# Where the key and query norms of a cross-attention stand: beside the mixer's output projection and the second query block

## The chip, the cores and the metric

The kernel runs on one core of a Trainium2 chip. The metric is the device time of one execution in microseconds, the median of several runs. Below, PE is TensorE, DVE is VectorE, ACT is ScalarE, POOL is GpSimd and SP is SyncE, which only issues loads here.

## What is computed

Two transformer blocks on 256 tokens of width 1024, in float32. Each has two layers. The change touches the second block alone, and there one step of each layer: the cross-attention to a memory of 256 rows, with the projection that ends the mixer ahead of it.

```python
def mem_cross_attention(h, mem_n, w_q, w_kv, q_gain, k_gain, w_out):
    q = rmsnorm_2((h @ w_q).reshape(Bn, S, X_HEADS, X_HEAD_DIM), q_gain)
    k, v = jnp.split(mem_n @ w_kv, 2, axis=-1)
    k = rmsnorm_2(k.reshape(Bn, M, X_HEADS, X_HEAD_DIM), k_gain)
    s = jnp.einsum('bqhd,bkhd->bhqk', q, k) * (X_HEAD_DIM ** -0.5)
    ...
for l in range(DEPTH):
    x = x + mixer(h)                      # ends with  @ w_out, "mix_out"
    x = x + mem_cross_attention(rmsnorm_2(x, norm_mem_q[l]), rmsnorm_2(mem, norm_mem_kv[l]), ...)
    x = x + swiglu(rmsnorm_2(x, norm_ffn[l]), ffn_w_gu[l], ffn_w_down[l])
```

There are 4 heads of width 256, so each head's keys (and queries) fill two tiles of 128 rows by 256 tokens, and a head's norm sums the squares of both.

## The kernel before, in words

**Weights and tiles.** Every weight matrix is streamed in blocks of 1024 x 512 (2 MB) into `raw`, which has two slots. A block is cut in four quarters. ACT copies a quarter to `w_hi` (`split_high`, L1406), rounded to a shorter format; DVE subtracts to get the remainder `w_lo` (`split_low`, L1927). One output tile (128 columns by 256 tokens) is 24 matmuls: 8 parts of the inner dimension times three products of high and low parts (`tile_t`, L602). A quarter of the next block may overwrite `w_hi` only when the tile that used the quarter is summed, so `split_high(b + 1, t)` waits for tile t of block b. SP loads block b when `split_low` of block b-2 is complete, since they share a slot.

**Order.** There is no scheduler. Each engine runs its own list, written out by hand, strictly in order, and the engines meet at semaphores. An instruction that waits holds up all that stands behind it on its engine.

**The steps in question**, for each layer of the second block:

1. `mix_out`, two blocks, 8 tiles. For each tile DVE adds the tile to `hidden` (`add_tile`, L1978), ACT writes the high part of the normed operand and the squares (`finish_chunk`, L1424 and L1428) and then splits a quarter (L1406); DVE writes the low part (`finish_low`, L1947) and splits.
2. `xq`, first block, 4 tiles. The token norm is summed on PE after two of them (L674), ACT turns it into `rs`, and DVE scales the tiles into `xq`.
3. `xq`, second block, 4 tiles, with the four key norms between them.
4. the four query norms, with nothing between.
5. attention: 8 units of scores, softmax, transposes and values; then `x_out`.

**One head norm** (`head_norms`) is a chain over four engines: ACT squares a head's two tiles (`square`, L1453, 128x512), PE sums them (`hn_sum`, L698), ACT takes Ln and Exp (`scale`, L1463 and L1466), DVE scales the two tiles (L1999). On ACT the list is square(0), and then for each i: square(i+1), scale(i), `between(i)`. On PE it is hn_sum(i), `between(i)`; on DVE scale(i), `between(i)`. What `between` issues is how other work is put beside the norms.

The scores of the attention wait until all norms of queries and keys are scaled (`hn_scaled`).

## Time and profile before

| | us |
|---|---|
| median of 3 runs | 1709.52 (1707.77 to 1711.32) |
| the profiled execution | 1702.04 |
| its span | 1700.3 |
| PE busy | 1604.6 (94%) |
| DVE busy | 1128.2 (66%) |
| ACT busy | 807.7 (48%) |
| layer 0: first tile of `mix_out` read, to the first tile of `x_out` read | 965.45 to 1044.25 |
| layer 1: the last tile of the first `xq` block read, to the first tile of `x_out` read | 1436.14 to 1481.37 |

All positions are microseconds from the start of the span. The profiled execution is 7.5 us quicker than the median of the runs, so a sum made in the trace is carried to the median as a difference. PE is the busy engine and DVE and ACT have room, which makes the places where PE stands still the ones to look at.

### The profile page before, as it was taken

Reading aid. Unit: us, or ns where it says so; the run is one execution under the profiler, and the core shown is the slowest. Engines: PE = TensorE matmul, PEld = TensorE weight load, DVE = VectorE, ACT = ScalarE, POOL = GpSimd, SP = SyncE. Lnnn points to the kernel's source line nnn. Section 1 sums busy time; section 2 is a strip of 40 time slices with the busy share of each in tenths; the row PEclk is TensorE's granted clock in tenths of the full one; section 3 lists DMA queues with packets and bytes.
Section 4 is the critical chain, followed back from the end, with each engine's and each line's share of the span. In section 5 each row is a group of like instructions: output and inputs, shape, how many; then the busy total and the mean of one; then the engine's idle time right before and its main releaser. Section 6 shows DMA issues by size and latency. Waiting matters only on the chain.

```text
span 1700.3 us, 31460 instructions
## 1 busy us (share of the span) xinstructions
PE 1604.6 (94%) x12572; PEld 1523.9 (90%) x12572; DVE 1128.2 (66%) x2032; ACT 807.7 (48%) x1402; POOL 188.7 (11%) x200
## 2 busy tenths in 40 slices
PE   6988999999998899999998989999989999899998
PEld 5876898999997699999996688999989999899997
DVE  5884644777675667777677755666677566566666
ACT  4446225444354554445554455544455555554443
POOL 2670501000031020002000011000020002010000
PEclk9998898999999999999998799999999999999999
DMA  6420002454553045544542142555535444256552
GB/s 212 148 81 20 1 2 96 152 180 166 183 189 132 1 149 199 197 171 176 194 153 99 50 150 80 169 199 198 171 114 188 141 158 152 75 171 199 186 174 88
DMA packets 125813, 236.56 MB, mean 139 GB/s; under 512 B 2614, under 2 KB 50025, under 8 KB 125689
## 3 DMA queue, kind: packets, MB, share of 16 engines
q1 hardware_dynamic: 124393, 230.29, 39.2%
q0 software_dynamic: 1296, 4.53, 0.8%
q8 instruction: 89, 1.46, 0.4%
q14 instruction: 35, 0.29, 0.1%
HBM read 233.76 MB, written 1.05 MB: 138 GB/s over the span
## 4 chain that ended last, share of the span: by engine, by line
PE 83%; DVE 10%; ACT 3%; issue 2%; SPq 0%; DMA 0%; POOL 0%; DVEq 0%; ACTq 0%; POOLq 0%
PE ps L602 46%; PE ps L649 6%; PE ps L648 6%; PE ps L647 6%; PE ps L610 5%; DVE w_lo L1927 3%; PE ps L780 3%; PE ps L741 2%; PE ps L698 2%; PE ps L929 1%; PE ps L754 1%; PE ps L911 1%; DVE u_lo L1947 1%; DVE hidden L1978 1%; ACT w_hi L1406 1%
## 5 line engine op out<-in xcount | busy, mean ns | idle before, releaser
L1406 ACT ACTIVATE w_hi<-raw 128x1024 fp32r<-128x1024 f32 x440 | 460.2, 1051 | 291.8 <-PE ps L649 137.3
L1927 DVE TENSOR_TENSOR w_lo<-raw,w_hi 128x1024 fp32r<-128x1024 f32 x440 | 540.7, 1229 | 10.4 <-ACT w_hi L1406 10.2
L602 PE MATMUL ps<-u_hi,w_hi 128*128 128x256 f32 (+1 forms) x1544 | 446.9, 289 | 14.9 <-DVE u_lo L1947 8.6
L602 PE MATMUL ps<-u_hi,w_lo 128*128 128x256 f32 (+1 forms) x1544 | 440.8, 285 | 0.0
L602 PE MATMUL ps<-u_lo,w_hi 128*128 128x256 f32 (+1 forms) x1544 | 440.4, 285 | 0.0
L602 PEld LDWEIGHTS ps<-u_hi,w_hi 128*128 128x128 f32 x1544 | 294.4, 191 | 21.6 <-DVE u_lo L1947 10.6
L602 PEld LDWEIGHTS ps<-u_hi,w_lo 128*128 128x128 f32 x1544 | 294.8, 191 | 0.0
L602 PEld LDWEIGHTS ps<-u_lo,w_hi 128*128 128x128 f32 x1544 | 293.8, 190 | 0.5
L602 PE MATMUL ps<-a_hi,w_hi 128*128 128x256 f32 (+1 forms) x800 | 230.0, 288 | 5.3 <-DVE a_lo L1942 2.3
L602 PE MATMUL ps<-a_lo,w_hi 128*128 128x256 f32 (+1 forms) x800 | 227.2, 284 | 0.0
L602 PE MATMUL ps<-a_hi,w_lo 128*128 128x256 f32 (+1 forms) x800 | 227.1, 284 | 0.0
L647 PE MATMUL ps<-a_hi,w_hi 128*128 128x256 f32 (+1 forms) x688 | 195.1, 284 | 0.8 <-DVE hidden L1978 0.8
L649 PE MATMUL ps<-a_hi,w_lo 128*128 128x256 f32 (+1 forms) x688 | 195.6, 284 | 0.0
L648 PE MATMUL ps<-a_lo,w_hi 128*128 128x256 f32 (+1 forms) x688 | 195.3, 284 | 0.0
L1978 DVE TENSOR_TENSOR hidden<-ps,hidden 128x256 f32<-128x256 f32 (+1 forms) x272 | 115.9, 426 | 116.5 <-PE ps L649 60.5
L602 PEld LDWEIGHTS ps<-a_hi,w_hi 128*128 128x128 f32 x800 | 152.9, 191 | 7.3 <-DVE a_lo L1942 2.8
L1966 DVE TENSOR_TENSOR work<-ps,rs 128x256 f32<-128x256 f32 (+1 forms) x153 | 65.4, 428 | 140.6 <-PE ps L602 119.7
L602 PEld LDWEIGHTS ps<-a_hi,w_lo 128*128 128x128 f32 x800 | 153.2, 191 | 0.0
L602 PEld LDWEIGHTS ps<-a_lo,w_hi 128*128 128x128 f32 x800 | 152.2, 190 | 0.4
L647 PEld LDWEIGHTS ps<-a_hi,w_hi 128*128 128x128 f32 x688 | 129.9, 189 | 1.0 <-DVE w_lo L1927 1.0
L649 PEld LDWEIGHTS ps<-a_hi,w_lo 128*128 128x128 f32 x688 | 130.0, 189 | 0.0
L648 PEld LDWEIGHTS ps<-a_lo,w_hi 128*128 128x128 f32 x688 | 129.3, 188 | 0.0
(377 smaller groups left out, 2359.6 us busy)
## 6 DMA issues: line engine op xcount, KB each, us to landing
raw<-in_w_ff_dram SPq DMA_DIRECT2D x32, 2048.0 KB, 8.5
raw<-in_ffn_w_gu_dram SPq DMA_DIRECT2D x44, 1024.0 KB, 7.5
raw<-in_ffn_w_down_dram SPq DMA_DIRECT2D x10, 2048.0 KB, 7.8
raw<-in_xa_w_kv_dram SPq DMA_DIRECT2D x8, 2048.0 KB, 8.0
raw<-in_od_w_in_dram SPq DMA_DIRECT2D x6, 2048.0 KB, 8.0
raw<-in_w_in_ab_dram SPq DMA_DIRECT2D x5, 2048.0 KB, 7.8
raw<-in_ev_w_in_dram SPq DMA_DIRECT2D x5, 2048.0 KB, 8.1
raw<-in_xa_w_q_dram SPq DMA_DIRECT2D x4, 2048.0 KB, 7.8
```

What stands on the lines that cost most here:

```text
L602: mm = pe.matmul(bank[:, 0:n], wx[:, q, k * P:(k + 1) * P], x[ux][:, k, ts], start=k == 0 and i == 0, stop=k == KD - 1 and i == 2)
L610: mm = pe.matmul(bank[:, at:at + n_quarters * n].rearrange("p (q n) -> p q n", n=n), x[ux][:, k, ts], wx[:, q:q + n_quarters, k * P:k * P ...
L647: pe.matmul(tile_bank[t % 4][:, 0:n], hi[:, k, cols], a[0][:, at_k, ts], start=k == 0, stop=False)
L648: pe.matmul(tile_bank[t % 4][:, 0:n], hi[:, k, cols], a[1][:, at_k, ts], start=False, stop=False)
L649: mm = pe.matmul(tile_bank[t % 4][:, 0:n], lo[:, k, cols], a[0][:, at_k, ts], start=False, stop=k == chunks - 1)
L698: mm = pe.matmul(banks[u_ % 2][:, 0:n], matrix, hn_sq[:, u_ % 2, i * n:(i + 1) * n], start=i == 0, stop=i == tiles - 1)
L741: mm = pe.matmul((b4, b5)[v % 2][0:x["nq"], 0:x["nk"]], q, k, start=c == 0, stop=c == len(x["q"]) - 1)
L780: mm = pe.matmul(bank[x["parts"], r * P:r * P + x["nq"]], vs[r], at_pt[0:rows, v % 2, c, 0:x["nq"]], start=c == 0, stop=c == len(x["keys"] ...
L1406: act.activation(quarter(w_hi, b, q), raw_quarter(b, q), ACT.Copy).then_inc(high_split, 1)
L1927: dve.tensor_tensor(quarter(w_lo, b, q), raw_quarter(b, q), quarter(w_hi, b, q).bitcast(F32), ALU.subtract)\
L1966: dve.tensor_tensor(target, tile_bank[t][:, 0:n], rs[:, ts] if scale is None else scale, ALU.mult)\
L1978: dve.tensor_tensor(hidden[:, k, ts], tile_bank[t][:, 0:ts.stop - ts.start], hidden[:, k, ts], ALU.add)\
```

## The change

Three lists are edited alike, those of PE, ACT and DVE. The key norms move from the second `xq` block to `mix_out`: after the first tile of `mix_out`, the key norms are issued with the other seven tiles between them, two, two, two and one. The second `xq` block now has the query norms beside it: its first tile is issued, then the query norms with one tile behind the first of them and two behind the second; nothing stands behind the third and fourth. The arithmetic is the same, and no instruction is added or removed.

```diff
+        def mix_fill(i):
+
+            return 2 * i + 1, min(2 * i + 3, 8)
+
+        def xq_fill(i):
+
+            return ((1, 2), (2, 4), (4, 4), (4, 4))[i]
...
 (PE)
-                out_product(f"mix_out{layer}", REAL, ready)
-                b = first_of(f"xq{layer}")
-                block_t(b, u, REAL, ready=chunks_ready(), norm=REAL)
-
-                head_norms([(2, SEQ, ones)] * 4, between=lambda t: tile_t(b + 1, t, u, REAL))
-                head_norms([(2, SEQ, ones)] * 4)
+                mix_tiles(0, 1)
+                head_norms([(2, SEQ, ones)] * 4, between=lambda i: mix_tiles(*mix_fill(i)))
+                block_t(first_of(f"xq{layer}"), u, REAL, ready=chunks_ready(), norm=REAL)
+                second_tiles(0, 1)
+                head_norms([(2, SEQ, ones)] * 4, between=lambda i: second_tiles(*xq_fill(i)))
                 pe.wait_ge(hn_scaled, hn[0])
...
 (ACT)
-                residual(f"mix_out{layer}", f"memq{layer}", REAL)
+                def mix_tiles(lo, hi):
+                    for n in range(lo, hi):
+                        b, t = phases[f"mix_out{layer}"].first + n // 4, n % 4
+                        finish_chunk(n, f"memq{layer}", (tile_read, tile_at[b] + t + 1), REAL)
+                        split_high(b + 1, t)
+
+                def second_tiles(lo, hi):
+                    for t in range(lo, hi):
+                        split_high(phases[f"xq{layer}"].first + 2, t)
+
+                mix_tiles(0, 1)
+                pair_norms(xk, f"xkv{layer}", lambda i: mix_tiles(*mix_fill(i)))
                 norm_rs(rs[:, REAL], SEQ)
                 stream(f"xq{layer}", nothing, 0, 1)
-                for x, name, fill in ((xk, "xkv", True), (xq, "xq", False)):
-                    first, after = tile_at[phases[f"{name}{layer}"].first], phases[f"xq{layer}"].first + 2
...
-                               between=(lambda t: split_high(after, t)) if fill else None)
+                second_tiles(0, 1)
+                pair_norms(xq, f"xq{layer}", lambda i: second_tiles(*xq_fill(i)))
...
 (DVE)
-                residual(f"mix_out{layer}", f"memq{layer}", REAL)
-                rms_ready()
+                def mix_tiles(lo, hi):
+                    for n in range(lo, hi):
+                        b, t = phases[f"mix_out{layer}"].first + n // 4, n % 4
+                        add_tile(n, t, tile_at[b] + t, REAL)
+                        if n >= 1:
+                            finish_low(n - 1, f"memq{layer}", REAL)
+                        split_low(b + 1, t - 1)
...
+                mix_tiles(0, 1)
+                pair_norms(xk, "xa_k", lambda i: mix_tiles(*mix_fill(i)))
+                finish_low(KD - 1, f"memq{layer}", REAL)
+                rms_ready()
+                stream(f"xq{layer}", project_xq, 0, 1)
+                second_tiles(0, 1)
+                pair_norms(xq, "xa_q", lambda i: second_tiles(*xq_fill(i)))
```

How the lists come out is shown at two places. First ACT at the start of `mix_out` in layer 0. `u_hi<-hidden` and `squares<-hidden` are `finish_chunk`, `w_hi<-raw` is `split_high`, `work<-mx` is `square`, and the two `work` rows behind it are `scale`. Before:

```order
L1424 ACTIVATE u_hi<-hidden,gains 128x256 [waits tile_read]
L1428 ACTIVATE squares<-hidden 128x256 [waits sum_added]
L1406 ACTIVATE w_hi<-raw 128x1024 [waits tile_summed,raw_in1]
L1424 ACTIVATE u_hi<-hidden,gains 128x256 [waits tile_read]
L1428 ACTIVATE squares<-hidden 128x256 [waits sum_added]
```

and in the changed kernel, whose lines stand 15 further down:

```order
L1439 ACTIVATE u_hi<-hidden,gains 128x256 [waits tile_read]
L1443 ACTIVATE squares<-hidden 128x256 [waits sum_added]
L1421 ACTIVATE w_hi<-raw 128x1024 [waits tile_summed,raw_in1]
L1468 ACTIVATE work<-mx 128x512 [waits hn_summed,tile_read] x2
L1478 ACTIVATE work<-ps,cst 128x256 [waits hn_scaled,hn_summed]
L1481 ACTIVATE work<-work 128x256 [waits hn_ln]
L1439 ACTIVATE u_hi<-hidden,gains 128x256 [waits tile_read]
```

The squares of the first two heads' keys now stand behind the chunk and the quarter of the first tile. On PE the sum that needs them stands between the first tile and the second (`work,cst` is `hn_sum`):

```order
L610 MATMUL ps<-a_hi,w_hi 128x256 [waits operand_split]
L610 MATMUL ps<-a_lo,w_hi 128x256
L610 MATMUL ps<-a_hi,w_lo 128x256
L706 MATMUL ps<-work,cst 128x256 [waits hn_ln,hn_squared]
L706 MATMUL ps<-work,cst 128x256
L610 MATMUL ps<-a_hi,w_hi 128x256 [waits tile_read,low_split]
```

Before, the fourth row followed directly on the third of a tile, with the waits `tile_read,low_split`; now PE first waits for the squares.

The second place is ACT from the first `xq` block to the query norms, layer 0. Before:

```order
L1406 ACTIVATE w_hi<-raw 128x1024 [waits tile_summed,raw_in1]
L1406 ACTIVATE w_hi<-raw 128x1024 [waits tile_summed] x3
L1453 ACTIVATE work<-mx 128x512 [waits hn_summed,tile_read] x2
L1463 ACTIVATE work<-ps,cst 128x256 [waits hn_scaled,hn_summed]
L1466 ACTIVATE work<-work 128x256 [waits hn_ln]
L1406 ACTIVATE w_hi<-raw 128x1024 [waits tile_summed,raw_in0]
```

and now:

```order
L1421 ACTIVATE w_hi<-raw 128x1024 [waits tile_summed,raw_in1]
L1421 ACTIVATE w_hi<-raw 128x1024 [waits tile_summed] x3
L1421 ACTIVATE w_hi<-raw 128x1024 [waits tile_summed,raw_in0]
L1468 ACTIVATE work<-mx 128x512 [waits hn_summed,tile_read] x2
L1478 ACTIVATE work<-ps,cst 128x256 [waits hn_scaled,hn_summed]
L1481 ACTIVATE work<-work 128x256 [waits hn_ln]
```

The row with `raw_in0` is the first quarter of the next weight, `x_out`: it waits for the load of that block. It stood behind the first norm's squares, and stands ahead of them now.

## Rows read from the trace of the kernel before

**Rows 1.** The page, busy time by engine: us, share of the span, instructions.

```profile
PE 1604.6 (94%) x12572; PEld 1523.9 (90%) x12572; DVE 1128.2 (66%) x2032; ACT 807.7 (48%) x1402; POOL 188.7 (11%) x200
```

**Rows 2.** The page, the chain that ended last, shares by engine.

```profile
PE 83%; DVE 10%; ACT 3%; issue 2%; SPq 0%; DMA 0%; POOL 0%; DVEq 0%; ACTq 0%; POOLq 0%
```

**Rows 3.** Timeline of DVE, layer 0: start, us, line, tile [idle before <- releaser].

```profile
965.45 0.42 DVE L1978 TENSOR_TENSOR hidden<-ps,hidden 128x256 f32<-128x256 f32 x1 [1.76 <-PE ps L602]
...
985.33 0.42 DVE L1978 TENSOR_TENSOR hidden<-ps,hidden 128x256 f32<-128x256 f32 x1 [0.89 <-PE ps L602]
...
997.82 0.42 DVE L1966 TENSOR_TENSOR mx<-ps,rs 128x256 f32<-128x256 f32 x1 [0.23 <-PE ps L602]
...
1001.58 0.88 DVE L1999 SCALAR_TENSOR_TENSOR mx<-mx,late,work 128x256 f32<-128x256 f32 x2 [2.20 <-ACT work L1466]
1003.45 0.42 DVE L1966 TENSOR_TENSOR mx<-ps,rs 128x256 f32<-128x256 f32 x1 [0.99 <-PE ps L602]
...
1014.57 0.42 DVE L1966 TENSOR_TENSOR mx<-ps,rs 128x256 f32<-128x256 f32 x1 [0.92 <-PE ps L602]
...
1022.32 0.88 DVE L1999 SCALAR_TENSOR_TENSOR mx<-mx,late,work 128x256 f32<-128x256 f32 x2 [0.45 <-ACT work L1466]
...
1044.25 0.42 DVE L1978 TENSOR_TENSOR hidden<-ps,hidden 128x256 f32<-128x256 f32 x1 [1.99 <-PE ps L602]
```

**Rows 4.** Timeline of ACT, layer 0.

```profile
966.63 1.04 ACT L1406 ACTIVATE w_hi<-raw 128x1024 fp32r<-128x1024 f32 x1
...
997.82 1.06 ACT L1406 ACTIVATE w_hi<-raw 128x1024 fp32r<-128x1024 f32 x1 [1.78 <-PE ps L602]
998.78 1.13 ACT L1453 ACTIVATE work<-mx 128x512 f32<-128x512 f32 x2
```

**Rows 5.** Timeline of PE, layer 0.

```profile
988.21 0.39 PE L602 MATMUL ps<-u_hi,w_hi 128*128 128x256 f32 x1 [0.44 <-DVE u_lo L1947]
...
999.45 1.13 PE L698 MATMUL ps<-work,cst 128*128 128x256 f32 x4 [1.67 <-ACT work L1453]
...
1023.25 5.52 PE L741 MATMUL ps<-mx 128*128 128x256 f32 x16 [1.93 <-DVE mx L1999]
```

**Rows 6.** The load of `x_out`'s first block, layer 0: issue, time to landing, and DMA share (second to last column) around its end.

```profile
994.68 0.37 SPq L566 DMA_DIRECT2D raw<-in_xa_w_out_dram  x1
```

```profile
raw<-in_xa_w_out_dram SPq DMA_DIRECT2D x1, 2048.0 KB, 7.8
```

```profile
1000.00:1002.00 2.00, 2.00 (x17) 1.95 (x16) 0.42 (x2) 0.89 (x2) 0.00 (x0) 1.00 0.94 347
```

**Rows 7.** The same steps in layer 1: timeline of DVE, and the chain.

```profile
1436.14 0.42 DVE L1966 TENSOR_TENSOR mx<-ps,rs 128x256 f32<-128x256 f32 x1 [0.23 <-PE ps L602]
...
1481.37 0.43 DVE L1978 TENSOR_TENSOR hidden<-ps,hidden 128x256 f32<-128x256 f32 x1 [1.96 <-PE ps L602]
```

```profile
1461.57 1.14 PE ps L741 x4
```

**Rows 8.** PE after its longer waits (timeline), and granted clock (third to last column) of windows.

```profile
19.19 0.56 PE L602 MATMUL ps<-u_hi,w_hi 128*128 128x272 f32 x1 [4.20 <-DVE w_lo L1927]
...
542.35 0.56 PE L685 MATMUL ps<-cst,rs_mem 128*128 128x128 f32 x2 [2.47 <-ACT rs_mem L1438]
...
922.75 0.49 PE L741 MATMUL ps<-mx 64*128 64x128 f32 x4 [3.10 <-DVE mx L2010]
...
1347.82 0.39 PE L602 MATMUL ps<-a_hi,w_hi 128*128 128x256 f32 x1 [2.04 <-DVE a_lo L2533]
```

```profile
18.00:22.00 4.00, 2.81 (x12) 2.84 (x13) 3.20 (x3) 2.40 (x3) 3.02 (x5) 1.00 1.04 310
542.00:544.00 2.00, 1.28 (x4) 0.86 (x5) 0.16 (x1) 0.91 (x3) 0.00 (x0) 0.63 0.00 0
924.00:926.00 2.00, 1.50 (x5) 0.98 (x5) 1.89 (x5) 0.91 (x4) 0.00 (x0) 0.70 0.00 0
1348.00:1352.00 4.00, 4.00 (x22) 4.00 (x23) 0.00 (x0) 3.37 (x3) 0.00 (x0) 0.57 0.00 0
1024.00:1028.00 4.00, 4.00 (x12) 2.97 (x12) 1.43 (x5) 1.13 (x4) 0.00 (x0) 0.60 0.00 0
```

More of the change, by code:

```diff
@@ L1365, in _ @@
                     u, a = a, u
-                out_product(f"mix_out{layer}", REAL, ready)
-                b = first_of(f"xq{layer}")
-                block_t(b, u, REAL, ready=chunks_ready(), norm=REAL)
-                head_norms([(2, SEQ, ones)] * 4, between=lambda t: tile_t(b + 1, t, u, REAL))
-                head_norms([(2, SEQ, ones)] * 4)
+                def mix_tiles(lo, hi):
+                    for n in range(lo, hi):
+                        tile_t(first_of(f"mix_out{layer}") + n // 4, n % 4, a, REAL, ready if n == 0 else None)
+                def second_tiles(lo, hi):
+                    for t in range(lo, hi):
+                        tile_t(first_of(f"xq{layer}") + 1, t, u, REAL)
+                mix_tiles(0, 1)
[3 more added lines that the diff above has]
+                head_norms([(2, SEQ, ones)] * 4, between=lambda i: second_tiles(*xq_fill(i)))
                 pe.wait_ge(hn_scaled, hn[0])
@@ L2714, in _, with mix_tiles, second_tiles, pair_norms @@
                                gate=[lr[:, c] for c in range(8)], ts=REAL, between=lambda i: memory_tiles(*od_fill(i)))
-                residual(f"mix_out{layer}", f"memq{layer}", REAL)
-                rms_ready()
+                def mix_tiles(lo, hi):
+                    for n in range(lo, hi):
+                        b, t = phases[f"mix_out{layer}"].first + n // 4, n % 4
[3 more added lines that the diff above has]
+                        split_low(b + 1, t - 1)
                 def project_xq(i, t, gt):
                     scaled(xq[:, 4 * i + t], t, gt, REAL)
-                def second_xq(t):
-                    b = phases[f"xq{layer}"].first + 1
-                    project_xq(1, t, tile_at[b] + t)
-                    split_low(b + 1, t - 1)
-                stream(f"xq{layer}", project_xq, 0, 1)
-                for x, g, between in ((xk, "xa_k", second_xq), (xq, "xa_q", None)):
+                def second_tiles(lo, hi):
+                    for t in range(lo, hi):
+                        b = phases[f"xq{layer}"].first + 1
+                        project_xq(1, t, tile_at[b] + t)
+                        split_low(b + 1, t - 1)
+                def pair_norms(x, g, between):
                     head_norms([([x[:, 2 * h + r] for r in range(2)], [col(g, 2 * layer + r) for r in range(2)],
                                  [x[:, 2 * h + r] for r in range(2)]) for h in range(4)], between=between)
+                mix_tiles(0, 1)
[5 more added lines that the diff above has]
+                pair_norms(xq, "xa_q", lambda i: second_tiles(*xq_fill(i)))
                 attention([dict(nq=P, nk=SEQ, kind=None, parts=slice(0, P), chunks=slice(2 * h, 2 * h + 2),
```

8 lines of the change are left out of this document (6 added, 2 removed).

## The prediction

> **What bounds the kernel now.** I read the page first. PE is busy 94% of the span [rows 1], and the chain that ended last lies on PE for 83% of its length, with 10% on DVE and 3% on ACT [rows 2]. So what this change can win is PE time that stands idle or runs slowly between the mixer's projection and the attention, and what it can lose is the same. After that I read the timelines of DVE, ACT and PE of that stretch in layer 0, and compared the same stretch of layer 1.
>
> The clearest clock of PE's progress is when DVE reads a finished tile. I call that moment R. In `mix_out` the first tile is read at 965.45 and the eighth at 985.33 [rows 3]: 19.88 / 7 = 2.84 us a tile, without a pause. In the second `xq` block the first tile is read at 1003.45 and the fourth at 1014.57 [rows 3]: 11.12 / 3 = 3.71 us for a tile with a key norm's sum ahead of it. One sum between tiles thus costs 0.87 us when its squares are ready.
>
> When they are not ready PE waits. The last tile of the first `xq` block is read at 997.82; ACT splits a quarter at the same moment, starts the squares 0.96 us later at 998.78 [rows 4], and PE starts the sum at 999.45, 0.67 us after that and after an idle 1.67 us [rows 5]. The next tile is read 4.00 us after the sum's start, at 1003.45. The same wait comes once more before the query norms. After the last tile is read at 1014.57, the four query norms run alone. The last scaling starts at 1022.32 and the attention at 1023.25 [rows 3, 5], 0.93 us later. From 1014.57 that is 8.68 us in which PE does little. From the read at 997.82 to the attention it is 25.43 us, and in layer 1 from 1436.14 to 1461.57 also 25.43 us [rows 7]. The two layers are alike.
>
> **The change, part by part.** I count for one layer, in the trace's own time.
>
> *Tiles beside the key norms.* The first tile of `mix_out` is read at R. ACT's quarter for it starts at 966.63, which is R + 1.18 [rows 3, 4], and the order puts the key squares behind it: they start at R + 1.18 + 0.96 = R + 2.14, and PE can start the sum at R + 2.14 + 0.67 = R + 2.81. Until then PE has nothing else, since its list has the sum ahead of the second tile. The second tile is read 4.00 us after the sum starts, at R + 6.81 instead of R + 2.84: **+3.97**. The other three sums find their squares ready, because ACT makes them one head ahead, and cost 0.87 each: **+2.61**. Their own scale steps on ACT and DVE take about 1 us each and lie beside two tiles of 2.84. DVE gets to the tile behind a scaling up to 0.7 us late and has caught up by the next; four banks of PSUM cover that. So the last of the eight tiles is read 6.58 us later than now.
>
> Behind it PE waits for the last low part of the operand: 0.44 us today [rows 5]. The last scaling delays DVE by about 0.2 us more there: **+0.2**. If DVE and ACT were later than I follow them, this term would grow to about 1 us. The other bound is -0.4, if the wait were gone. The four key sums themselves are not new work: they leave the second `xq` block, which is counted next.
>
> *Query norms beside the second `xq` block.* Counted from the read at 997.82. The first tile of the second block needs no sum ahead of it any more and is read at 1000.66. Now the order matters again: ahead of the query squares ACT has the first quarter of `x_out`, which waits for that tile and for its load. The load is issued at 994.68 and lands 7.8 us later [rows 6], at 1002.48; the DMA engines are 94% busy until 1002. Today nobody sees this, since the quarter is wanted at 1003.5 only. The issue does not move relative to 997.82, because it hangs on the fourth quarter of the first `xq` block. So the quarter starts at 1002.48, the squares at +0.96, the sum at +0.67: 1004.11. PE has been idle since 1000.6, for 3.5 us. Then the reads: 1004.11 + 4.00 = 1008.11, + 3.71 = 1011.82 with the second sum, + 2.84 = 1014.66 for the fourth tile. The third sum follows at once. The last head's squares stand behind that tile's quarter on ACT: the last sum starts at 1014.66 + 0.96 + 0.67 = 1016.29. From a sum's start to the scaling on DVE it is 2.13 us (999.45 to 1001.58 [rows 3, 5]), and 0.93 more to the attention: 1016.29 + 2.13 + 0.93 = 1019.35. Against 1023.25: **-3.90**. Most of it is the tail behind the last tile, 4.69 us instead of 8.68, less the longer wait at the head.
>
> The Trainium skill bears on the landing: its page "DMA: Bandwidth & Descriptors", section "Anatomy of one DMA — SWDGE (gpsimd) path", fits 2.0 us fixed plus bytes over 436 GB/s for a load issued from GpSimd. For 2 MB that would be an estimated 6.8 us by that page, a landing 1.0 us sooner and a sum lower by 1.0 us a layer. These loads are issued by SP and take 7.8, and I go by the row.
>
> *Sum without the clock.* +3.97 + 2.61 + 0.2 - 3.90 = +2.9 a layer, **+5.8** for both.
>
> *The clock.* The change turns two waits of 1.67 us a layer into one of 2.8 and one of 3.5, both with dense tiles behind. What such a wait does to the granted clock can be read elsewhere in this trace. After a wait of 3.10 us the window from 924 has 0.70; after 2.47 us the one from 542 has 0.63; after 2.04 us four microseconds from 1348 have 0.57 in dense tiles; after 4.20 us at the start of the program the clock stays at 1.00 [rows 8]. So three of these four waits were followed by a stretch at the lower level, 1.2 instead of 2.4 GHz. The price in dense tiles is 4.0 x 0.43 = 1.7 us. Four new waits in the two layers, three of them punished: **+5.1**; the bounds are 0 and +6.9. One dip may go: in layer 0 the attention begins at 0.60 [rows 8] and takes 21.00 us from its start to the first `x_out` tile (1023.25 to 1044.25), in layer 1 without a dip 19.80 (1461.57 to 1481.37) [rows 3, 5, 7]. Less stands still ahead of it now, so I take it away: **-1.2**; the bounds are -1.2 and +1.2, the latter if layer 1 gets one.
>
> Total: +5.8 + 5.1 - 1.2 = **+9.7 us**. The profiled execution goes from 1702.04 to about 1711.7, and the median from 1709.52 to 1719.2; I say 1719.
>
> **The rivals.** All times are on the median's scale. About 0.2%, 3.4 us, is what a measurement of this kernel can tell from no change.
>
> *No dip comes.* The waits of 1.67 us in this stretch leave the clock alone today, and the longer ones may be spared as well, as the wait of 4.20 us was. Then only the order counts: +5.8 - 1.2 = +4.6, 1714. For it: a wait of 1.93 us led to a dip in layer 0 and not in layer 1. Against it: three of four.
>
> *Every wait is punished, and the attention's dip stays.* +5.8 + 6.9 = +12.7, 1722. In this kernel it means that the second `mix_out` tile and the second tile of the second `xq` block both run at 0.5 in both layers. [...]
>
> *The load is not late.* If the `x_out` block has landed by 1000.66, the wait at the head of the query norms is 1.8 us shorter, as long as today's, and brings no dip. For that the landing would have to take 6 us instead of 7.8. Then +5.8 - 3.6 = +2.2, with about one dip left at `mix_out` and the attention's gone: +2.7, 1712, no measurable change. The DMA row speaks against it.
>
> *Faster: the sums find their squares.* If PE does not stand at the two new places, because ACT gets to the squares before PE ends the tile ahead, each of the two places costs only 0.87 for a sum. That takes 3.97 - 0.87 = 3.1 away at `mix_out` and 3.65 at `xq` (the sum at 1000.46 instead of 1004.11): 2.9 - 6.75 = -3.9 a layer, and 1709.5 - 7.7 - 1.2 = 1701. It decides from the point where the two waits together are 2.9 us shorter a layer than I find. Against it stands the order: on ACT both squares come behind work that waits for that very tile.
>
> *The change does nothing*: excluded, the order has it on all three engines.
>
> **How the numbers follow.** Forecast, two or three dips, +8 to +10: 0.50. No dip, 1714: 0.20. All dips, 1722: 0.14. The load not late, 1712: 0.10. Faster, 1701: 0.06. The first three are slower by more than 3.4 us: 0.84; same 0.10; faster 0.06. The range reaches from 1711, which takes in the case without dips and half of the next, to 1726, which has all dips, the +1 of the operand's wait in both layers and a spread of the runs of about 2. What is left out is the faster case, half of the one with an early load, and 0.05 above.
>
> **What would show it.** In the changed profile, in both layers: (1) a wait of PE of about 2.8 us behind the first `mix_out` tile, ended by ACT's squares, and 26.5 us from the first to the eighth read instead of 19.9; (2) a wait of about 3.5 us behind the first tile of the second `xq` block, ended by the same line, with ACT itself waiting for the load of `x_out`; (3) 4.7 us from the last `xq` tile's read to the attention instead of 8.7, and 21.5 us instead of 25.4 from the read ahead of the block; (4) clock windows below 1.0 behind most of the waits. I am wrong if the wait at (1) is under 2 us, if ACT doesn't wait for the load at (2), or if later stages give the time back, for which I see no slack since PE is dense behind the attention.

## The result

| | before | changed |
|---|---|---|
| median | 1709.52 us (1705.08 to 1713.9, 7 runs) | 1724.79 us (1718.66 to 1726.82, 7 runs) |
| ratio | 1 | 1.0079, 95% interval 1.0059 to 1.0098 |
| profiled execution | 1702.04 | 1726.82 |

The change costs 0.8%: 15.3 us between the medians. The prediction was 1719 in a range of 1711 to 1726.

The page of the changed kernel begins with these lines: its span, the busy time by engine, and, further down, the chain that ended last.

```profile
span 1725.0 us, 31460 instructions
...
PE 1618.4 (94%) x12572; PEld 1536.4 (89%) x12572; DVE 1128.1 (65%) x2032; ACT 809.4 (47%) x1402; POOL 188.8 (11%) x200
...
PE 81%; DVE 11%; ACT 3%; issue 2%; DMA 1%; SPq 0%; POOL 0%; DVEq 0%; ACTq 0%; POOLq 0%
```

The instructions are as many as in [rows 1]. DVE and ACT are as busy as they were. PE is busy 13.8 us longer with the same work, at a lower clock (the windows below show where), and the chain now has 1% on a DMA where [rows 2] had 0%. The clock and the load are the two places where the sizes differ from the forecast; the order of the engines' work went as worked out.

**The wait in `mix_out`.** The timeline of PE shows the waits of over a microsecond, first in layer 0, then in layer 1 (start, us, line, tile, count, [idle before <- releaser]; L706 is the sum that was L698).

```profile
978.27 1.15 PE L706 MATMUL ps<-work,cst 128*128 128x256 f32 x4 [2.83 <-ACT work L1468]
...
1022.57 1.13 PE L706 MATMUL ps<-work,cst 128*128 128x256 f32 x4 [3.70 <-ACT work L1468]
...
1039.33 5.48 PE L749 MATMUL ps<-mx 128*128 128x256 f32 x16 [1.93 <-DVE mx L2027]
...
1422.92 2.04 PE L706 MATMUL ps<-work,cst 128*128 128x256 f32 x4 [2.83 <-ACT work L1468]
...
1468.28 2.07 PE L706 MATMUL ps<-work,cst 128*128 128x256 f32 x4 [4.62 <-ACT work L1468]
...
1486.22 1.99 PE L749 MATMUL ps<-mx 128*128 128x256 f32 x8 [1.93 <-DVE mx L2027]
```

Both layers wait 2.83 us behind the first `mix_out` tile, ended by ACT's squares (L1468). The second wait was forecast at 3.5 and is 3.70 and 4.62. The wait of 1.93 ahead of the attention is that of [rows 5].

The timeline of DVE in layer 0 can be compared with [rows 3]: the first, second and eighth tile of `mix_out`, the last of the first `xq` block, the four of the second, the last scaling, and the first tile of `x_out`.

```profile
975.48 0.42 DVE L2006 TENSOR_TENSOR hidden<-ps,hidden 128x256 f32<-128x256 f32 x1 [1.75 <-PE ps L610]
...
983.81 0.42 DVE L2006 TENSOR_TENSOR hidden<-ps,hidden 128x256 f32<-128x256 f32 x1 [2.51 <-PE ps L610]
...
1003.55 0.42 DVE L2006 TENSOR_TENSOR hidden<-ps,hidden 128x256 f32<-128x256 f32 x1
...
1016.07 0.42 DVE L1994 TENSOR_TENSOR mx<-ps,rs 128x256 f32<-128x256 f32 x1 [0.27 <-PE ps L610]
...
1018.90 0.42 DVE L1994 TENSOR_TENSOR mx<-ps,rs 128x256 f32<-128x256 f32 x1 [1.28 <-PE ps L610]
...
1028.09 0.42 DVE L1994 TENSOR_TENSOR mx<-ps,rs 128x256 f32<-128x256 f32 x1 [2.51 <-PE ps L610]
...
1034.63 0.42 DVE L1994 TENSOR_TENSOR mx<-ps,rs 128x256 f32<-128x256 f32 x1 [1.28 <-PE ps L610]
...
1038.39 0.88 DVE L2027 SCALAR_TENSOR_TENSOR mx<-mx,late,work 128x256 f32<-128x256 f32 x2 [0.45 <-ACT work L1481]
...
1060.18 0.42 DVE L2006 TENSOR_TENSOR hidden<-ps,hidden 128x256 f32<-128x256 f32 x1 [1.96 <-PE ps L610]
```

From the first to the eighth read it is 28.07 us, where it was 19.88. The second tile is read 8.33 us after the first and not 6.81: the missing 1.5 us are the clock. From the last `xq` read to the attention it is 1039.33 - 1034.63 = 4.70 us, against 8.68: the tail went as worked out. From 1016.07 to the attention it is 23.26, against 25.43.

**The load of `x_out`.** ACT's timeline at the head of the query norms, layer 0 and then layer 1, and the times from issue to landing of that block in layer 1 and in layer 0, can be compared with [rows 4] and [rows 6].

```profile
1020.94 1.06 ACT L1421 ACTIVATE w_hi<-raw 128x1024 fp32r<-128x1024 f32 x1 [3.81 <-DMA raw<-in_xa_w_out_dram]
1021.90 1.14 ACT L1468 ACTIVATE work<-mx 128x512 f32<-128x512 f32 x2
...
1466.65 1.06 ACT L1421 ACTIVATE w_hi<-raw 128x1024 fp32r<-128x1024 f32 x1 [4.72 <-DMA raw<-in_xa_w_out_dram]
```

```profile
raw<-in_xa_w_out_dram SPq DMA_DIRECT2D x1, 2048.0 KB, 8.9
...
raw<-in_xa_w_out_dram SPq DMA_DIRECT2D x1, 2048.0 KB, 8.0
```

ACT itself waits for the load, 3.81 and 4.72 us, with the squares queued behind the quarter. The sum on PE starts 0.67 us after the squares, as it did in [rows 4, 5]. The load took 8.0 us in layer 0 and 8.9 in layer 1. In the trace of before it took 7.8 and 7.9; why the one of layer 1 became longer isn't shown.

**The clock.** The granted clock is the third column from the end; the windows lie behind the five waits that were followed by a dip (the first three in layer 0).

```profile
978.00:984.00 6.00, 5.73 (x32) 5.62 (x33) 1.07 (x3) 1.64 (x4) 0.00 (x0) 0.72 0.93 344
...
1023.00:1029.00 6.00, 6.00 (x35) 5.82 (x34) 1.79 (x4) 1.84 (x4) 0.00 (x0) 0.72 0.79 301
...
1040.00:1045.00 5.00, 5.00 (x18) 3.81 (x17) 2.28 (x8) 1.70 (x6) 0.00 (x0) 0.66 0.00 0
...
1422.00:1428.00 6.00, 5.08 (x26) 4.72 (x27) 0.88 (x2) 2.28 (x5) 0.00 (x0) 0.72 0.84 303
...
1467.00:1475.00 8.00, 6.72 (x29) 6.33 (x30) 0.89 (x3) 2.65 (x6) 0.00 (x0) 0.57 0.67 254
```

6 x 0.28 = 1.7 us are lost in a window with 0.72, as much at 1040 (5 x 0.34), and twice as much, 8 x 0.43 = 3.4, in the last. All four new waits are followed by the lower of the two levels, 1.2 instead of 2.4 GHz, and in layer 0 the attention has its dip as before.

**Where the two profiled executions differ.** Their spans differ by 24.7 us, more than the medians. Cut at the first `mix_out` and the first `x_out` read of each layer, the difference is: ahead of layer 0's stretch +10.0 (965.45 to 975.48, in code that the change doesn't touch), layer 0's stretch +5.9 (78.80 to 84.70), between the stretches +0.4, layer 1's stretch +8.3 (77.60 to 85.94), behind it 0.0. The two stretches together are +14.2, and that is what stands beside the +15.3 of the medians. The first 10 us come up again in the last experiment.

### The profile page after: what moved, and what is told of

Read it like the earlier page. It is cut to its first block, busy times and chain, and to the rows that moved or that the text cites. A ratio compares the mean times of both kernels' runs of the same rounds, so it can differ in the third digit from the quotient of the medians.

```text
span 1725.0 us, 31460 instructions
## 1 busy us (share of the span) xinstructions
PE 1618.4 (94%) x12572; PEld 1536.4 (89%) x12572; DVE 1128.1 (65%) x2032; ACT 809.4 (47%) x1402; POOL 188.8 (11%) x200
## 4 chain that ended last, share of the span: by engine, by line
PE 81%; DVE 11%; ACT 3%; issue 2%; DMA 1%; SPq 0%; POOL 0%; DVEq 0%; ACTq 0%; POOLq 0%
PE ps L610 44%; PE ps L657 6%; PE ps L656 6%; PE ps L655 6%; PE ps L618 5%; DVE w_lo L1955 3%; PE ps L788 3%; PE ps L749 2%; PE ps L706 1%; PE ps L762 1%; PE ps L937 1%; DMA raw<-in_xa_w_out_dram 1%; PE ps L919 1%; ACT w_hi L1421 1%; DVE hidden L2006 1%
```

## The experiments

The theory: the order of ACT's list is what costs. Squares that are ready stand behind work that waits (for a tile, for a load), PE waits for them, and the clock dips behind each such wait. The rivals: that the relocation itself costs, through seven more places where sums, scalings and tiles share DVE and PSUM; that the load of `x_out` alone makes the second half bad; that the dips come whatever PE does in the waits.

All times are medians; a ratio is to the kernel before on the same chip. "Stretch" is the sum over both layers of the time from the first `mix_out` read to the first `x_out` read in the run's profile, less the 156.40 (78.80 + 77.60) of the kernel before.

| kernel | us | ratio (95%) | as us | stretch |
|---|---|---|---|---|
| changed kernel | 1724.79 | 1.0079 (1.0059 to 1.0098) | +13.5 | +14.2 |
| the same again | 1723.21 | 1.0081 (1.0054 to 1.0108) | +13.8 | +12.9 |
| key squares first | 1717.15 | 1.0025 (1.0005 to 1.0045) | +4.3 | +4.9 |
| query squares first | 1710.82 | 0.9993 (0.9976 to 1.0011) | -1.2 | +3.9 |
| both first | 1700.87 | 0.9944 (0.9924 to 0.9964) | -9.6 | -6.7 |
| waits filled | 1716.58 | 1.0043 (1.0023 to 1.0064) | +7.4 | +9.6 |
| half the load | 1714.54 | 1.0029 (1.0007 to 1.005) | +5.0 | +5.1 |
| keys' half alone | 1720.9 | 1.0059 (1.0038 to 1.0081) | +10.1 | +7.1 |
| both first, other fill | 1698.49 | 0.9941 (0.9918 to 0.9964) | -10.1 | -8.6 |
| old places, squares first | 1706.67 | 0.9969 (0.9948 to 0.999) | -5.3 | -7.2 |

"As us" is the ratio less 1, times 1709.5. The ratio is not the quotient of two medians, which would jump: of the 27 runs of the kernel before that stand beside the first four experiments, 13 lie between 1705.6 and 1709.9 and 14 between 1713.4 and 1715.8. The stretch of one profile lies within the interval of the ratio everywhere but for query squares first, where the profiled execution (1718.2) was the slowest of twelve.

### The changed kernel again

> The changed kernel as it is, beside the one before on the same chip. The stretch from the first mix_out tile's read to the first x_out tile's read was 78.8 and 77.6 us in the two layers before, 84.7 and 85.9 after; the first profile of after was also 10 us later before it came to any changed instruction. Theory (the two new waits and the clock behind them): the stretches again near 85 and 86, the same waits of 2.8 and 3.7 to 4.6 us, and the 10 us ahead of them gone or of either sign. Rival (the change also slows what is ahead of it): the 10 us are there again. Ratio to before 1.005 to 1.010.

The ratio comes out the same. The profile, of an execution of 1718.28, has the same order of work, but the dips lie otherwise: none behind the query norms' wait of layer 0, a single one (1.5 us) behind that of layer 1, and one in the attention of each layer (21.33 and 21.34 us to the first `x_out` read, where an attention without a dip takes 19.80). Its waits of PE in `mix_out` and at the query norms, layer 0:

```profile
973.41 1.13 PE L706 MATMUL ps<-work,cst 128*128 128x256 f32 x4 [2.83 <-ACT work L1468]
...
1017.28 1.13 PE L706 MATMUL ps<-work,cst 128*128 128x256 f32 x4 [3.29 <-ACT work L1468]
```

and the windows behind the one and the other:

```profile
974.00:978.00 4.00, 4.00 (x21) 3.95 (x20) 0.88 (x2) 0.89 (x2) 0.00 (x0) 0.57 1.02 388
1017.00:1022.00 5.00, 4.72 (x33) 4.52 (x34) 1.60 (x4) 2.36 (x5) 0.00 (x0) 1.00 1.00 371
```

The wait of 3.29 left the clock alone, the shorter one of 2.83 did not. So a wait's length does not by itself tell whether a dip follows, and the places of the dips differ between executions of one kernel. Without the dip the second tile of the block is read 7.26 us after the first and the attention starts 21.32 us after the last read of the first block; the prediction had 7.45 and 21.53.

### Key squares first

`begin` issues the first `mix_out` tile's work behind the squares of two heads. The keys are there by then, so nothing holds the squares up.

```diff
 (ACT)
-            def head_norms(units, between=None, **more):
+            def head_norms(units, between=None, begin=None, **more):
...
+                    if i == 0 and begin is not None:
+                        begin()
                     scale(i)
...
-                mix_tiles(0, 1)
-                pair_norms(xk, f"xkv{layer}", lambda i: mix_tiles(*mix_fill(i)))
+                pair_norms(xk, f"xkv{layer}", lambda i: mix_tiles(*mix_fill(i)), begin=lambda: mix_tiles(0, 1))
```

> Of the changed kernel one thing differs: on ACT the squares of the first two heads' keys stand ahead of the first mix_out tile's chunk and quarter, not behind them. Theory (PE waits for squares that stand behind the tile on ACT): the wait of 2.83 us behind the first mix_out tile is gone, and with it the clock's dip; the second tile is read 3.7 us after the first instead of 8.3 to 8.4; both stretches 4.7 us shorter than after's, about 80 and 81; 9 us less than after in all. Rival (the key norms crowd ACT and DVE beside the tiles, and these pace mix_out): under 1 us a layer is won, since the same instructions run there.

ACT's timeline around the first tile (read at 976.66), PE's next wait, and the windows of `mix_out` and behind that wait:

```profile
974.02 1.13 ACT L1468 ACTIVATE work<-mx 128x512 f32<-128x512 f32 x2
...
977.85 1.05 ACT L1421 ACTIVATE w_hi<-raw 128x1024 fp32r<-128x1024 f32 x1
```

```profile
1018.84 1.65 PE L706 MATMUL ps<-work,cst 128*128 128x256 f32 x3 [3.37 <-ACT work L1468]
```

```profile
976.00:1000.00 24.00, 24.00 (x192) 23.59 (x191) 16.28 (x28) 16.63 (x31) 7.57 (x7) 1.00 0.50 176
```

```profile
1018.00:1025.00 7.00, 6.16 (x25) 5.80 (x26) 0.88 (x2) 2.20 (x5) 0.00 (x0) 0.51 0.82 300
```

The squares run 2.6 us before the tile is read. PE is busy for all of the 24 us, at full clock, and the eight reads take 23.50 and 23.56 us: 19.88 and four sums of 0.9. The whole wait of 2.83 with its dip, 4.6 us a layer, came from two instructions in the wrong place of one list. The queries' wait stayed (3.37 and 4.51), and its dips were of the double kind (3.4 and 3.1 us in the windows) in both layers.

### Query squares first

On ACT the squares of the first two heads' queries and the first scale step stand ahead of `x_out`'s first two quarters, not behind the first.

```diff
 (ACT)
-                second_tiles(0, 1)
-                pair_norms(xq, f"xq{layer}", lambda i: second_tiles(*xq_fill(i)))
+                pair_norms(xq, f"xq{layer}", lambda i: second_tiles(*((0, 2), (2, 4), (4, 4), (4, 4))[i]))
```

> Of the changed kernel one thing differs: on ACT the squares of the first two heads' queries and the first scale step stand ahead of x_out's first quarter, not behind it. Theory (the squares wait behind a quarter that waits for its load): the wait of 3.7 and 4.6 us behind the first tile of the second xq block is gone, and the dip behind it; 5 to 7 us less in each stretch than after, about 79 and 79; 11 to 12 us less in all. Rival (the load itself paces this part): the wait only moves, to the quarter's next user, and under 1 us is won.

Waits of PE in layer 0's stretch, all that are over a microsecond, and DVE's reads of the first two tiles of the second `xq` block:

```profile
980.70 1.13 PE L706 MATMUL ps<-work,cst 128*128 128x256 f32 x4 [2.83 <-ACT work L1468]
...
1036.27 4.54 PE L749 MATMUL ps<-mx 128*128 128x256 f32 x12 [1.93 <-DVE mx L2026]
```

```profile
1021.33 0.42 DVE L1993 TENSOR_TENSOR mx<-ps,rs 128x256 f32<-128x256 f32 x1 [1.28 <-PE ps L610]
...
1025.04 0.42 DVE L1993 TENSOR_TENSOR mx<-ps,rs 128x256 f32<-128x256 f32 x1 [1.00 <-PE ps L610]
```

The second tile comes 3.71 us after the first, where it was 9.19 and 11.29. From the last read of the first block to the attention it is 17.78 us in both layers (23.26 and 25.35 in the changed kernel, 25.43 before). The load lands no earlier (7.7 and 8.9 us after its issue); it is just no longer in the squares' way. The medians differ by 12.4 us, the stretches by 9.0. Part of that gap is one dip of the double kind at the place that this edit doesn't touch: behind layer 1's wait of 2.83 us the second `mix_out` tile comes 9.58 us after the first instead of 8.33, with these windows.

```profile
1419.00:1424.00 5.00, 4.46 (x17) 4.10 (x18) 0.88 (x2) 1.90 (x4) 0.00 (x0) 0.50 0.94 316
1424.00:1430.00 6.00, 6.00 (x43) 5.90 (x43) 2.78 (x6) 2.14 (x4) 1.19 (x1) 0.87 0.25 89
```

 This is the larger of the two places by the medians, and its waits were the longer.

### Both first

Both edits.

> Both edits of e2 and e3 on the changed kernel. Theory: the gains add, stretches of about 74.6 and 73.7 us, 4 us a layer under the kernel before, so a ratio to before of 0.995 (0.993 to 0.998). That is the faster case of the prediction, 1701 us. Rival (something else holds the layer back, the clock or the tail): the second edit gives nothing on top of the first, and the ratio is 1.000 or more.

DVE's reads of the first two tiles of `mix_out`, and the window of PE over all of it, in layer 0:

```profile
969.41 0.42 DVE L2006 TENSOR_TENSOR hidden<-ps,hidden 128x256 f32<-128x256 f32 x1 [1.77 <-PE ps L610]
...
973.42 0.42 DVE L2006 TENSOR_TENSOR hidden<-ps,hidden 128x256 f32<-128x256 f32 x1
```

```profile
968.00:993.00 25.00, 25.00 (x201) 24.58 (x199) 16.55 (x29) 16.63 (x31) 7.57 (x7) 1.00 0.48 169
```

No wait over a microsecond is left between `mix_out` and the attention. The kernel is faster than before, by 0.56% (0.36 to 0.76). The two edits gave 8.0 and 9.0 us in the stretches when each was made alone (against the second profile of the changed kernel), and 19.6 together; the surplus of 2.6 us goes with the double dips that the profiles of the single edits have at the place left alone. The relocation is therefore not what costs: the same places for the norms, with ACT's list the other way round, win.

### Waits filled

PE gets 7 and 9 matmuls that nobody reads, on constants, in the two waits. Each counts as two in the timeline.

```diff
 (PE)
+                def keep_busy(n):
+                    for _ in range(n):
+                        pe.matmul(b6[:, 0:SEQ], ones, cst[:, 0:SEQ], start=True, stop=True)
+
                 mix_tiles(0, 1)
+                keep_busy(7)
...
                 second_tiles(0, 1)
+                keep_busy(9)
```

> The changed kernel with matmuls that nobody reads put where PE waits: 7 ahead of the first key norm's sum, 9 ahead of the first query norm's sum, about 0.34 us each. The waits stay, PE is only kept busy in them. Theory (the clock's dip is a price of its own, on top of the wait): no window under 1.0 behind the two places; mix_out takes 26.4 to 26.6 us from the first to the eighth read instead of 28.1; from the read ahead of the second xq block to the attention it is 21.3 to 22.6 us in both layers; stretches of about 81 to 83 us; 5 to 8 us less than after in all. Rival (the dips cost nothing, the waits are all): stretches as in after, 83 to 86, ratio to before 1.008.

PE's timeline behind the first `mix_out` tile, DVE's reads of the first two tiles, and the windows over both filled places and in the attention of layer 0 and of layer 1:

```profile
972.47 3.19 PE L1384 MATMUL ps<-cst 128*128 128x256 f32 x14
975.50 1.10 PE L706 MATMUL ps<-work,cst 128*128 128x256 f32 x4
```

```profile
972.67 0.42 DVE L2012 TENSOR_TENSOR hidden<-ps,hidden 128x256 f32<-128x256 f32 x1 [1.78 <-PE ps L610]
...
979.48 0.42 DVE L2012 TENSOR_TENSOR hidden<-ps,hidden 128x256 f32<-128x256 f32 x1 [1.00 <-PE ps L610]
```

```profile
974.00:982.00 8.00, 8.00 (x59) 7.55 (x58) 3.07 (x6) 4.60 (x8) 1.57 (x2) 1.00 0.78 264
1019.00:1026.00 7.00, 6.77 (x50) 6.56 (x51) 2.77 (x5) 3.95 (x8) 0.00 (x0) 1.00 0.62 237
1034.00:1038.00 4.00, 3.52 (x9) 2.77 (x10) 0.84 (x3) 0.56 (x2) 0.00 (x0) 0.57 0.00 0
1474.00:1482.00 8.00, 6.30 (x15) 5.00 (x16) 3.20 (x10) 2.14 (x7) 0.00 (x0) 0.57 0.00 0
```

The second read comes 6.81 us after the first, exactly what the prediction had for the order alone, and the eight reads take 26.61 us instead of 28.07. So 1.5 us a place are the clock's own share in `mix_out`, and none of the four filled places (two in each layer) has a dip. The ratio falls by 0.36% against the changed kernel's, with intervals that overlap a little. Not all of the gain arrives, since the attention now dips in both layers (21.34 and 22.06 us, undisturbed 19.80), in layer 1 by nearly twice as much as in layer 0. In layer 0 the load also took 9.0 us here, so that the attention starts 22.70 us after the last read of the first block; in layer 1 it took 7.7 and that is 21.66. Whether the dips in the attention come because those ahead of it didn't isn't shown: other runs have both.

### Half the load

The block of `x_out` is loaded with half of its rows, 1 MB. The other half of `x_out`'s product uses what `raw` held before.

```diff
-        add(f"x_out{layer}", [[cols(w["xa_w_out_2"][layer], c)] for c in (0, BLOCK)])
+        add(f"x_out{layer}", [[cols(w["xa_w_out_2"][layer], c, rows=slice(0, D // 2))] for c in (0, BLOCK)])
```

> The changed kernel, but x_out's two blocks load only the first 512 of their 1024 rows (1 MB instead of 2), so x_out is computed with stale weights in the other half; the order of all engines is after's. Theory (the wait ahead of the query norms is the load's landing): the load lands about 5.3 us after its issue, before the first tile of the second xq block ends; the read behind the first query norm's sum comes 5.6 us after the one ahead instead of 7.3 to 11.3; from the read ahead of the block to the attention 19.7 us. Rival (the wait is ACT's order alone, the load only happens to end then): unchanged.

The load's time to landing (all four blocks), and ACT and PE at the head of the query norms of layer 0:

```profile
raw<-in_xa_w_out_dram SPq DMA_DIRECT2D x4, 1024.0 KB, 4.9
```

```profile
1020.30 1.06 ACT L1421 ACTIVATE w_hi<-raw 128x1024 fp32r<-128x1024 f32 x1 [1.84 <-PE ps L610]
```

```profile
1021.92 1.13 PE L706 MATMUL ps<-work,cst 128*128 128x256 f32 x4 [1.73 <-ACT work L1468]
```

The quarter now waits for its tile and no longer for the load, the sum waits 1.73 us, and no dip follows in either layer. That is the prediction's rival of an early load, made true: the attention starts 19.76 us after the last read of the first block in both layers. The load, with the dips behind its wait, accounts for 3.5 and 5.6 of the changed kernel's 23.26 and 25.35 us; behind it a wait of 1.73 remains, which only the order takes away (17.78). The +5.1 that is left in the stretches has both dips at `mix_out` and one in the attention of layer 1 (20.90 us; 19.85 in layer 0).

### The keys' half alone

All three lists issue the second `xq` block whole, and the query norms alone behind it, as before; the key norms stay beside `mix_out`.

```diff
 (PE, ACT and DVE alike)
-                second_tiles(0, 1)
+                second_tiles(0, 4)
...
-                head_norms([(2, SEQ, ones)] * 4, between=lambda i: second_tiles(*xq_fill(i)))
+                head_norms([(2, SEQ, ones)] * 4)
```

> One part of the change alone: key norms beside mix_out as in after; the second xq block's four tiles in a row, and then the four query norms with nothing beside them, as before. Theory: mix_out 28.1 us with its wait of 2.83 and its dip; from the read ahead of the block to the attention 4 x 2.84 + 8.68 = 20.0 us, less than before's 25.4 and less than after's 21.3 to 25.4, because nothing waits for the load; stretches about 81.5 and 80.5; ratio to before 1.002 to 1.005, under after's. Rival (query norms beside tiles are worth their place): slower than after.

`mix_out` takes 28.05 and 28.23 us, the second block's tiles come 2.84 us apart with nothing between, the tail is 8.69 and 8.68 again. The attention starts 20.04 us after the last read of the first block. In the stretches that is +7.1 us, and 1.0059 came out, a little above what was expected; the attention dips in both layers here (20.85 and 21.29 us), which is part of it. So the keys' half costs 8.2 and 8.4 us in `mix_out` and gets 5.4 back in `xq`. The queries' half shortens the tail by 4.0, and still the attention starts 3.2 and 5.3 us later after that read in the changed kernel (23.26 and 25.35) than here: it loses more at its own head than it wins at the tail. In its repeated profile the same two differences are 1.3 and 4.1 us. The two ratios cannot tell it, since their intervals overlap.

### Both first, with another fill

As both first, and the four `x_out` quarters on ACT stand two, one, none, one behind the query norms: the last quarter stood ahead of the last head's squares and now stands behind its scale step.

```diff
 (ACT)
-                pair_norms(xq, f"xq{layer}", lambda i: second_tiles(*((0, 2), (2, 4), (4, 4), (4, 4))[i]))
+                pair_norms(xq, f"xq{layer}", lambda i: second_tiles(*((0, 2), (2, 3), (3, 3), (3, 4))[i]))
```

> e4_both_first with one more step on ACT: the last head's query squares stand ahead of the last quarter, which goes behind the last scale step. Theory: from the last xq tile's read to the attention 4.1 to 4.3 us instead of 4.69, 1 us less than e4 in all, a ratio to before of 0.993 to 0.995. Rival (the quarter then delays the attention's first exponent): as e4 or slower.

The tail is 4.20 us instead of 4.69, and the attention starts 17.29 and 17.30 us after the last read of the first block instead of 17.78. Half a microsecond a layer is less than the comparison of the whole can tell (0.9941 against 0.9944). It has the lowest ratio of all versions, 0.59% below the kernel before with an interval that ends at 0.36%, and can't be told from both first.

### The old places, squares first

Is it the new places that win, or the order? This is the kernel before, with ACT's list alone changed: the key squares ahead of the last quarter of the second `xq` block, and the first two query squares ahead of the last `x_out` quarter.

```diff
 (ACT)
+                for t in range(3):
+                    split_high(second, t)
...
+                key_square(0)
+                key_square(1)
+                split_high(second, 3)
+                for i in range(4):
+                    if 1 <= i < 3:
+                        key_square(i + 1)
+                    key_scale(i)
+                    if i == 3:
+                        query_square(0)
+                        query_square(1)
+                    split_high(second + 1, i)
+                for i in range(4):
+                    if 1 <= i < 3:
+                        query_square(i + 1)
+                    query_scale(i)
```

> The kernel before, without the change. One thing differs, on ACT alone: the squares of the first two heads' keys stand ahead of the last quarter of the second xq block, and those of the first two heads' queries ahead of the last quarter of x_out. Theory (the norms' place is worth little, ACT's order is worth the time): both waits of 1.67 us go, from the read ahead of the second xq block to the attention 25.4 becomes 21.7 us, stretches of 74 to 75 us with mix_out at 19.9; ratio to before 0.994 to 0.997, within 1 us a layer of e4. Rival (the norms must stand beside mix_out to win): 1.000, since the waits only move down the list.

ACT's timeline around the last read of the first block:

```profile
1007.69 1.14 ACT L1453 ACTIVATE work<-mx 128x512 f32<-128x512 f32 x2
...
1009.56 1.06 ACT L1406 ACTIVATE w_hi<-raw 128x1024 fp32r<-128x1024 f32 x1 [0.73 <-PE ps L602]
```

The squares are written before that tile is read at 1009.56, so the two waits of 1.67 us in [rows 5] are gone, the tail is 6.83 instead of 8.68, and the attention starts 21.65 and 22.05 us after the last read instead of 25.43. That gives 0.31% (0.10 to 0.52) without moving a norm. With the norms moved as well it is 0.59% (0.36 to 0.82). The intervals overlap, and the stretches differ by 1.4 us over both layers: what the relocation adds is small and not shown by these runs.

### The kernel before, again

The kernel before was profiled once more, unchanged, for the 10 us ahead of the first stretch.

> The kernel before, unchanged, for a second profile. The first mix_out tile of layer 0 was read at 965.5 in its first profile and at 967.9 to 977.9 in those of eight other kernels, whose instructions are the same up to there. Theory (this is the spread of runs, with the clock's dips in the earlier stages): a time above 967 here too, and stretches of 78.8 and 77.6 us within 1.5, the attention's dip aside. Rival (the change slows the stages ahead of it): 965.5 again.

This execution took 1706.9 us. Its stretches are 78.81 and 77.61 us, the first profile's to 0.01. But its first `mix_out` tile is read at 970.10, not at 965.45. Over the twelve profiles that moment lies between 965.45 and 977.90, in code that is the same in all of them. It doesn't sort them by kernel: the two profiles of the changed kernel have it at 975.48 and 970.61, and of the three fast kernels two have it early (967.90 and 969.41) and one late (old places, squares first: 977.20). It follows the clock lost in the first 965 us (1 less the granted clock, times the time): 42.7 and 46.0 us in the two profiles of before, 52.6 in the first of the changed kernel, 41.0 (967.90) and 58.5 (977.20) in two of the fast ones. So this part is a scatter between executions, and not shown to be the change's. What sets these early dips stays open.

## Why the prediction was right, and where its numbers were off

The sign and the range were right, and so was the mechanism: ACT's squares behind a waiting quarter, at both places. That 1724.8 lies inside the range is in part luck: it is 1.2 us from the upper end, the dips and the landing were both taken too low, and what had stretched the range that far, up to 1 us a layer for the operand's wait and 2 for the spread of the runs, is not what came. By the prediction's steps:

**The first wait and `mix_out`.** Forecast 2.8, measured 2.83 in all ten layers that had it. The second read at R + 6.81: with the wait filled and the clock up, 6.81. The eight reads should take 19.88 + 3.97 + 2.61 = 26.46 us; at full clock they took 26.61. The operand's wait, put at +0.2, came to +0.03 (1003.55 to 1016.07 is 12.52, [rows 3] give 12.49). These two misses nearly cancel.

**The second block.** The tail: 4.69 forecast, 4.70 and 4.69 measured. The whole at full clock: 21.53 forecast, 21.32 in the repeated profile. What was off is the landing of the load. I took layer 0's 7.8 us for both layers, as the trace of before had it (7.8 and 7.9); it was 8.0 and 8.9, and the sum's wait 3.70 and 4.62 instead of 3.5. Taking the clock's share out by the rows of the repeated profile (7.26 us to the second read with a wait of 3.29, so 7.67 and 8.59 with 3.70 and 4.62, where 9.19 and 11.29 were measured), the layers gain 3.69 and 2.78 instead of 3.90 each. The order's own sum is then 6.73 + 0.03 - 3.69 and 6.72 + 0.03 - 2.78, together **+7.0** for a forecast of +5.8.

**The clock.** This is the term that was mis-sized. I had three of the four new waits punished, and the attention's dip of layer 0 gone: 5.1 - 1.2 = +3.9. In the profile all four were punished, the last doubly, and the attention kept its dip: (28.07 - 26.61) + (28.23 - 26.60) + 1.52 + 2.70 - 0.11 for the attention = **+7.2**. In the repeated profile it was three of four. The price of 1.7 us a dip was right in most windows, and about 1.5 of it reached the path; that one can cost twice as much I hadn't counted. "Three of four" left out rows of the same trace: 4.30 us ahead of 88.09 (0.57 in the 4 us behind), 2.19 ahead of 141.88 (0.65 and 0.50 from 142 to 150) and 2.14 ahead of 69.19 (1.00). With them it is five of seven, so the estimate stands. But in front of dense tiles a wait of 1.80 us ahead of 497.33 was followed by 0.57 as well, while the 1.67 of this stretch never were, so the length alone decides nothing there either. That the attention's dip would go because less stands still ahead of it was a reason without a row. Of the 24 layers profiled, 16 have one there, always behind the same wait of 1.93 us, also where no wait over a microsecond stood before it (both first: 1024 to 1028 at 0.57).

**The sum.** +7.0 + 7.2 = +14.2, the two stretches of the first profile; in the second they were +12.9. Forecast was +9.7, and +15.3 was measured between the medians.

**The rivals.** "No dip comes" fell in both profiles. "Every wait is punished, and the attention's dip stays", 1722, is what the first profile shows; it had a chance of 0.14. The Trainium skill's page "TensorE: Matmul & The Clock Gate", section "HAM oscillation — how this bites in real kernels", tells of a kernel whose matmuls waited some 3 to 5 us for a DMA between bursts, and in which each burst behind such a wait began at the half clock. Of the six waits here of about that length (3.29 to 4.62 us, at the query norms) five agree, and the one of 3.29 does not; the ten of 2.83 us are shorter and were all followed by the lower clock. "The load is not late" was made true with half the load: +5.0, while I had +2.7, since I had counted one dip at `mix_out` and two came (+1.4), and the attention's dip, which I had taken away, was there once (+1.1). "The sums find their squares" I put at 1701 as something the order excludes. It does; with the order changed that kernel takes 1700.87, or 1699.9 by its ratio. The agreement hides that its attention kept its dips, where I had counted -1.2.

**The observations asked for.** (1) The wait of 2.83 us came in both profiles of the changed kernel; the eight reads took 28.07 to 28.23 us there and not 26.5, which they took only with the waits filled (26.61). (2) ACT waited for the load in both profiles of the changed kernel, and with the key squares first and the waits filled: eight layers, 3.40 to 4.77 us. (3) The tail was 4.7 us, but from the read ahead of the block it was 23.26 and 25.35 us (21.32 and 24.11 in the second profile) where I had 21.5. (4) Windows below 1.0 stood behind four and three of the four waits. None of the signs that would have made it wrong appeared, and the time behind the stretches was not given back: 218.93 us before from layer 1's first `x_out` read to the end of the span, 218.94 after.

## What to carry to other kernels

When a step is put between the tiles of another, look on each in-order engine for the small instruction on which the bottleneck engine will wait, and put it ahead of all work that waits for the tile just computed or for a load; here that order was worth 1.4% of the kernel with the norms in the same places. What the move adds once the order is right, these runs can't tell. Pulling a consumer of a weight forward means counting from the load's issue, and with some reserve: the same load landed 7.8 and 7.9 us after its issue before, and 8.9 in layer 1 after. And each new wait of some 3 us ahead of dense matmuls should be priced with the clock's dip behind it (about 1.5 us here, behind 15 of 16 such waits), while a dip that is already there should not be counted as going without a reason.

## What the runs showed of the hardware

- Waits of 2.83 us behind a `mix_out` tile were followed by a lower clock ten times in ten, once with nearly twice the loss on the path (9.58 us to the second tile, where 8.33 was usual and 6.81 is the time without a dip); waits at the query norms' head of 3.29 to 4.62 us five times in six, three of these with twice the loss (up to 3.4 us); waits of 1.67 and 1.73 us in this stretch never; the wait of 1.93 us ahead of the sparse attention in 16 of 24 layers.
- With matmuls on constants that nobody reads in the two waits, the granted clock was 1.00 at all four filled places of one profile.
- The load of 2 MB at this one place of the program took 7.6 to 9.1 us to its landing (22 of them, in eleven profiles), that of 1 MB 4.9 (two).
- The same instructions reach the first `mix_out` tile up to 12.5 us earlier or later from one execution to another (965.45 to 977.90), and the clock lost there (41.0 to 58.5 us) goes with it. Ten microseconds of difference between two profiles can be nothing of the change.
